# The sample rows of a decoder step: ranked over 128 partitions and finished inside the last step

## The reference, cut to what matters

```python
def peer(h, w_pq, sub_keys, u_tab, v_tab):       # 8 heads, 128 keys a side, 16384 experts
    q = (xc @ w_pq).reshape(n, 8, 2, 128)
    s = einsum('nhpd,pkd->nhpk', q, sub_keys)
    s1, i1 = top_k(s[:, :, 0], 16);  s2, i2 = top_k(s[:, :, 1], 16)
    cand = s1[..., :, None] + s2[..., None, :]   # 16 x 16 candidates a head
    top_s, pos = top_k(cand, 16)                 # 16 experts a head, 128 a token
    eid = take(i1 * 128 + i2, pos)
    g = softmax(top_s)
    act = gelu(einsum('nhkd,nd->nhk', u_tab[eid], xc))
    return einsum('nhk,nhkd->nd', g * act, v_tab[eid])

def finish(x, mixed, p, ...):
    x = x + mixed @ w_out
    x = x + peer(rmsnorm(x, norm_ffn), ...)
    gate = sigmoid(rmsnorm(x, norm_ple) @ w_ple_gate)
    return x + (p @ w_ple_proj) * gate
```

## Time and profile before

| | us |
|---|---|
| median of 3 runs (lowest, highest) | 3370.78 (3368.08, 3371.01) |
| the profiled execution | 3372.78 |
| its span, first to last instruction | 3371.1 |
| busy: DVE, PE, POOL, ACT | 2623.5, 2566.4, 1997.2, 634.9 |
| gathers (queue 0): bytes, share of 16 engines | 1082.26 MB, 80.9% |

### The profile page before, as it was taken

The page is one execution under the profiler, slowest core; times in us unless marked ns, Lnnn a source line. Parts: engine busy times, 40 slices in busy tenths (PEclk is TensorE's granted clock), DMA queues, the critical chain, the costliest instruction groups (busy, mean ns, idle before and its releaser), DMA issues.

```text
span 3371.1 us, 27956 instructions
## 1 busy us (share of the span) xinstructions
PE 2566.4 (76%) x7838; PEld 1250.0 (37%) x7838; DVE 2623.5 (78%) x5916; ACT 634.9 (19%) x1411; POOL 1997.2 (59%) x2104
## 2 busy tenths in 40 slices
PE   6898998277778777877787678767867776778768
PEld 3555545134334333433343333333433333333323
DVE  4889894988887878787878887788778877897843
ACT  2332323111111111111111111111111111121101
POOL 1000000677777777777777777777777777777672
PEclk8999998589889898989899989998998899999889
DMA  6010004899999999999999999999999999999994
GB/s 202 19 38 19 31 30 188 319 392 410 411 411 404 411 411 407 405 411 405 403 403 411 407 404 409 411 408 400 405 411 407 400 411 411 405 400 408 408 357 185
DMA packets 318210, 1144.81 MB, mean 340 GB/s; under 512 B 37648, under 2 KB 41360, under 8 KB 317040
## 3 DMA queue, kind: packets, MB, share of 16 engines
q0 software_dynamic: 297216, 1082.26, 80.9%
q1 hardware_dynamic: 20856, 60.93, 5.0%
HBM read 1133.85 MB, written 10.72 MB: 340 GB/s over the span
## 4 chain that ended last, share of the span: by engine, by line
DMA 30%; DVE 18%; POOL 17%; PE 10%; issue 8%; ACT 0%; DVEq 0%; POOLq 0%
DMA arena<-in_peer_v_dram,arena 24%; POOL arena L1078 17%; DVE arena L1327 6%; DMA arena<-in_peer_u_dram,arena 6%; PE VA L1503 6%; PE QB L1537 3%; DVE XP L1339 2%; DVE arena L1257 2%; DVE arena L1254 2%; DVE arena L1261 1%; DVE arena L1292 1%; DVE arena L1295 1%; DVE arena L1296 1%; PE QB L1483 1%; PE QB L1586 0%
## 5 line engine op out<-in xcount | busy, mean ns | idle before, releaser
L1503 PE MATMUL VA<-arena 128*128 128x512 f32 x3032 | 1628.0, 677 | 689.4 <-DMA arena<-in_peer_v_dram,arena 563.4
L1327 DVE CUSTOM_DVE_ANT_0 arena<-arena,HP 128x1024 f32<-128x1024 f32 x1024 | 1231.3, 1219 | 496.5 <-DMA arena<-in_peer_u_dram,arena 492.3
L1078 POOL DMA_INDIRECT arena<-in_peer_u_dram,arena x1032 | 990.5, 960 | 399.1 <-issue 273.5
L1078 POOL DMA_INDIRECT arena<-in_peer_v_dram,arena x1032 | 985.1, 955 | 388.5 <-issue 261.9
L1503 PEld LDWEIGHTS VA<-arena 128*128 128x128 f32 x3032 | 603.7, 214 | 1620.7 <-issue 1300.0
L1151 ACT ACTIVATE arena<-ident,arena 128x128 f32<-128x128 f32 x758 | 279.9, 396 | 1194.9 <-PE VA L1503 1188.2
L1339 DVE SCALAR_TENSOR_TENSOR XP<-arena,XP 128x1024 f32<-128x1024 f32 x258 | 332.0, 1287 | 31.7 <-DMA arena<-in_peer_v_dram,arena 24.5
L1483 PEld LDWEIGHTS QB<-arena 128*128 128x128 f32 x2304 | 268.2, 192 | 34.6 <-issue 34.6
L624 DVE SCALAR_TENSOR_TENSOR arena<-arena 128x128 f32<-128x128 f32 x960 | 273.4, 348 | 7.9
L414 POOL COPY arena<-arena 128x1024 f32<-128x1024 f32 x8 | 8.3, 1042 | 452.9 <-DVE arena L644 452.9
L1483 PE MATMUL QB<-arena 128*128 128x128 f32 x2304 | 268.6, 275 | 2.6 <-PEq L191 2.6
(11 more groups left out here) (185 smaller groups left out, 1360.4 us busy)
## 6 DMA issues: line engine op xcount, KB each, us to landing
arena<-in_peer_u_dram,arena POOLq DMA_INDIRECT x1032, 11.2
arena<-in_peer_v_dram,arena POOLq DMA_INDIRECT x1032, 11.2
arena<-x SPq DMA_DIRECT2D x17, 512.0 KB, 6.8
arena<-in_x_prompt_dram SPq DMA_DIRECT2D x16, 512.0 KB
arena<-in_peer_wq_dram SPq DMA_DIRECT2D x8, 1024.0 KB, 14.1
arena<-in_w_in_dram SPq DMA_DIRECT2D x8, 896.0 KB, 12.7
x<-arena SPq DMA_DIRECT2D x8, 512.0 KB
arena<-in_w_ple_gate_dram SPq DMA_DIRECT2D x1, 4096.0 KB, 17.2
```

The source lines that it names most:

```text
L1078: nc.gpsimd.indirect_dma_start(rows[slot(turn)], None, table, bass.IndirectOffsetOnAxis(ap=index, axis=0)).then_inc(landed[slot(turn)], 16)
L1327: nc.vector.tensor_tensor_reduce(out=row, in0=row, in1=HP[:, :], scale=1.0, scalar=0.0, op0=ALU.mult, op1=ALU.add, accum_out=dots[:, t % 2 ...
L1503: last = nc.tensor.matmul(VA[:, c:c + BANK], diag[:, n % DIAGS, :], rows[slot(turn)][:, c:c + BANK], start=v_turn(t, k) == 0, stop=v_turn( ...
```

## The change

It has four parts, all in `experts`.

1. The samples are ranked with 64 lists a side (8 tokens times 8 heads) on 128 partitions. PE makes the queries as 8-column products, four groups at `j` = 16, 19, 22, 25; one key score product a side; one ACT copy each; then one `best16` over 128 partitions, a DMA that brings the second side's lists to the first 64 partitions (`s_second`), and pairs, names and gates on 64 partitions. `idxT` is asked for at `U_SAMPLE` = 62 of step 7 in place of 114.
2. The samples' v gathers and their whole finish move from the tail into step 7 (`V_SAMPLE` = 78), as do tile 7's p turn and ple product. SP stores tile 6 and loads x of tile 7 after the samples' small DMAs in place of before them.
3. The rms scale: x is turned and multiplied without it, and the scale goes into the sigmoid's `scale`. DVE's 128x1024 scaling goes, and the finish of a tile stands 7 choices earlier.
4. Tile 7's sigmoid, product, sum and store run in two halves of 512 columns. In the tail DVE takes the odd v rows in place of the even ones.

```diff
-RANK_SAMPLE_AT = (16, 34, 68, 84)
-U_SAMPLE, V_SAMPLE = 114, 92
+U_SAMPLE, V_SAMPLE = 62, 78
-    return k % 2 == 0 if t == LAST and k >= CHOICES - LAG else k % 4 == 0
+    return k % 2 == 1 if t == LAST and k >= CHOICES - LAG else k % 4 == 0
...
 # SP
-                store(t - 1)
-                sp.wait_ge(y_stored, t * 16)
-                load_x(t)
-                load_p(SAMPLE if t == LAST else t)
+                else:
+                    store(t - 1)
+                    sp.wait_ge(y_stored, t * 16)
+                    load_x(t)
+                    load_p(t)
...
+            sp.wait_ge(sq_ready, PARTS)
             for n in range(NB):
                 sp.dma_start(h_bc[:, n, :], h_dram[n].partition_broadcast(P)).then_inc(hbc_landed, 16)
+            sp.wait_ge(s_listed, 1)
+            sp.dma_start(s_second[0:SLISTS, :], s_lists[SLISTS:2 * SLISTS, :]).then_inc(s_second_landed, 16)
+            sp.wait_ge(s_chosen_ready, 1)
+            sp.dma_start(choice_dram.rearrange("b (h k) -> (b h) k", k=TOPK), s_chosen[0:SLISTS, :]).then_inc(s_stored, 16)
             sp.wait_ge(s_stored, 2 * 16)
             sp.dma_start(idxT, choice_dram.rearrange("n c -> c n"), ...)
...
+            store(LAST - 1)
+            sp.wait_ge(y_stored, LAST * 16)
+            load_x(LAST)
+            load_p(SAMPLE)
             load_p(LAST)
             store(SAMPLE)
+            for half in range(2):
+                cols = slice(half * BANK, (half + 1) * BANK)
+                sp.wait_ge(half_ready, half + 1)
+                sp.dma_start(y_prompt[0, LAST * P:SEQ, cols], xf[:, cols]).then_inc(y_stored, 16)
...
 # ACT
+            def gate_half(half):
+                cols = slice(half * BANK, (half + 1) * BANK)
+                act.wait_ge(fin_ready, 2 * order(LAST) + 1 + half)
+                act.wait_ge(rstd_ready, order(LAST) + 1)
+                nc.scalar.activation(h3[:, cols], QB[:, cols], ACT.Sigmoid, scale=rstd2).then_inc(half_sig, 1)
...
 # DVE
-                nc.vector.tensor_scalar(h3[0:R, :], x_rows(f, R), rstd2[0:R, :], None, ALU.mult).then_inc(h3_ready, 1)
+                nc.vector.reciprocal(rstd2[0:R, :], rms2[0:R, :]).then_inc(rstd_ready, 1)
+            def sample_lists():
+                dve.wait_ge(ssc_copied, 1)
+                best16(scores[:, 0:1, 0:NKEY], values.unsqueeze(1), s_top_i.unsqueeze(1), 1, None)
+                nc.vector.tensor_copy(indices, s_top_i).then_inc(s_listed, 1)
+            def sample_pairs():                                   # at j == 38
+                dve.wait_ge(s_second_landed, 16)
...
+                best16(s_cand.unsqueeze(1), s_best.unsqueeze(1), s_best_i.unsqueeze(1), 1, None)
...
+            def finish_half(half):
+                dve.wait_ge(half_sig, half + 1)
+                steps.link(TT(ple[:, cols], ple[:, cols], h3[:, cols], ALU.mult))
+                TT(xf[:, cols], xf[:, cols], ple[:, cols], ALU.add).then_inc(half_ready, 1)
...
 # PE
+            def sample_queries(p):                                # at j == 16 + 3 * p
+                pe.wait_ge(hT_copied, SAMPLE + 1)
+                for m in range(p * LISTS, (p + 1) * LISTS):
+                    for k in range(KD):
+                        last = nc.tensor.matmul(QB[:, m * NB:(m + 1) * NB], wq[k][:, m * P:(m + 1) * P], hT[:, k, 0:NB],
+                                                start=(k == 0), stop=(k == KD - 1))
...
-            turn_h3(LAST, P)
+            turn_x2(LAST, P)
             gate_products(LAST, P)
```

More of the change, by code:

```diff
@@ L83, in count_turns @@
                     su[b], n = n, n + 1
+            if t == LAST and j == V_SAMPLE:
+                for b in range(NB):
+                    sv[b], n = n, n + 1
             u[t, j], n = n, n + 1
@@ L1094, in _ @@
                             gather(peer_u, SU_TURN[n], idxT[:, n:n + 1])
+                    if t == LAST and j == V_SAMPLE:
+                        for n in range(NB):
+                            gather(peer_v, SV_TURN[n], idxT[:, n:n + 1])
                     gather_u(t, j)
@@ L1537, in gate_product, with sample_scores @@
                     last = nc.tensor.matmul(QB[0:R, c:c + BANK], h3T[:, k, 0:R], w_gate[:, k, c:c + BANK], start=(k == 0), stop=(k == KD - 1))
-                if c and first:
+                if first:
                     last.then_inc(fin_ready, 1)
+            def sample_queries(p):
[4 more added lines that the diff above has]
+                                                start=(k == 0), stop=(k == KD - 1))
+                last.then_inc(sq_ready, 1)
+            def sample_scores():
+                pe.wait_ge(sq_copied, 1)
+                for side in range(2):
+                    last = nc.tensor.matmul(QB[side * SLISTS:(side + 1) * SLISTS, BANK:BANK + NKEY], s_q[:, side * SLISTS:(side + 1) * SLISTS],
+                                            keysT[:, side, :], start=True, stop=True)
+                last.then_inc(ssc_ready, 1)
             def gate_products(f, R):
@@ L1570, in _ @@
[L1570 to L1571 removed]
+                            turn_x2(f, P)
                         for quarter in range(4):
[L1573 removed]
+                            if j == 49 + 2 * quarter:
                                 gate_product(f, P, quarter // 2 * BANK, quarter % 2 * (KD // 2))
+                    if t == LAST:
+                        for p in range(PARTS):
+                            if j == 16 + 3 * p:
+                                sample_queries(p)
+                        if j == 30:
+                            sample_scores()
+                        if j == V_SAMPLE:
+                            pe.wait_ge(cols_ready, 1)
+                            pe.wait_ge(fin_copied, LAST)
+                            for n in range(NB):
+                                turn = SV_TURN[n]
+                                pe.wait_ge(*landing(turn))
+                                for c in range(0, D, BANK):
+                                    last = nc.tensor.matmul(QB[0:NB, c:c + BANK], w_cols[:, n, :], rows[slot(turn)][:, c:c + BANK],
+                                                            start=(n == 0), stop=(n == NB - 1))
+                                last.then_inc(s_added, 1)
+                        if j == 84:
+                            turn_p(SAMPLE, NB)
+                        if j == 87:
+                            ple_product(SAMPLE, NB)
+                        if j == 92:
+                            turn_x2(SAMPLE, NB)
+                        for quarter in range(4):
+                            if j == 96 + 2 * quarter:
+                                gate_product(SAMPLE, NB, quarter // 2 * BANK, quarter % 2 * (KD // 2))
+                        if j == 110:
+                            turn_p(LAST, P)
+                        if j == 114:
+                            ple_product(LAST, P)
```

225 lines of the change are left out of this document (124 added, 101 removed).

## The result

The changed kernel takes 3375.14 us (median of 14 runs, 3370.54 to 3384.14); beside it the kernel before took 3369.85 (14 runs). The ratio is 1.0018, with a 95% interval from 1.0009 to 1.0026: five microseconds slower, where 21.8 less were forecast. The profiled execution took 3375.08, its span 3373.3.

A forecast was written before the change was run, and what follows sets the result against it. DMA engines at 411 GB/s bound the gathers, PE after about 3310. Last landing 3320.4 plus path 28.9 gives 3349.3 against the span of 3371.1, 21.8 less; 3370.8 - 21.8 = 3349, range 3343 to 3355.

The forecast's parts named there:

- The cluster's price: Step 7, choices 16 to 25: the samples' four query groups make PE 18.6 us late; loss 0 to 12.8 us, 5 taken.
- the broadcasts: Eight 512 KB transfers SP sends after the last query group; 10.2 us of DMA time, taken to keep the engines busy.
- the ring: The 13 row buffers, 16.6 us of gathers; a user of rows may be 5.8 us late before POOL stops.
- The step's own sum: Step 7, choices 16 to 25: PE needs 30 plus 11.9 us against 23.3 of arrivals, so is 18.6 late, less 5.8.
- the queries fall to 1.2 GHz: Rival: the samples' 8-column query products lower PE's clock; 256 passes take 63 us in place of 30, time 3382; chance 0.05.
- Steps 1 to 6 ... 0, with 6 to either side: Finish of steps 1 to 6, 7 choices earlier with one DVE scaling less: 0 us change, 6 to either side.
- no wait for the samples' list: Step 7, choice 62: the list is ready with 18 us to spare, so POOL's 8.41 us wait goes.
- The second lists: Rival: in step 7 their copy queues behind the broadcasts and DVE stops at choice 38; 5 us more, 3354; chance 0.10.
- PE is in time: Tail: PE has 20 rows, 35 us of work, within 51 us of gathers.
- The path after the last landing: End of the kernel, from the last gather's landing through the final store: 28.9 us, between 25 and 32.
- its loose term: The gate product in the last path, taken as 16.88 us; 32 passes are 13.90 at the full 2.4 GHz.

## Why the prediction was wrong, point by point

Two steps failed, one that was mis-sized and one that wasn't there. With the buffer at its old place and the clock kept up, the kernel takes 3349.13 us.

**The cluster's price ("the loss is between 0 and 12.8 us; I take 5, nearer to zero because of the broadcasts").** Mechanism and place were right: PE late with v rows behind four groups, the ring giving 5.8 us, POOL stopping for the rest. The size was wrong for two reasons. First, the durations came from rows at full clock, 0.117 and 0.125 us a pass. In this cluster a pass took 8.45/64 = 0.132 to 9.83/64 = 0.154 us, and the v rows between took 5.5 to 6.0 us a pair. The step's own sum with these rows: from 2954.22 to 3006.53 PE needs 52.3 us, against 9 x 2.58 = 23.2 of arrivals; it is 29.1 late, less 5.8 is 23.3, and the stretches show 21.5 lost. Second, the broadcasts covered nothing of the first three stops: SP issues them only when the last group is done,

```profile
3006.56 6.40 SPq L1063 DMA_DIRECT2D arena<-sample_h  x8
```

in the middle of the fourth. The sentence had said so itself ("SP sends when the last group is done") and took them for cover all the same. At full clock (64 columns, old place) the same sum is 2984.9 - 2945.9 = 39.0 less 23.2 less 5.8 = 10.0, and the stretches show 8.2. So at full clock the sum of this step holds, and 8.2 lies inside its 12.8; the 5 taken was too little, and the price of the clock came on top: 14.6 us by one pair of runs, 14.2 by the other.

**The rival "the queries fall to 1.2 GHz".** It named the cause, products of 8 columns, and had 0.05. The full price was too high: the granted clock went to 0.57 in the worst 10 us and to 0.67 to 0.77 over stretches of 25 that PE filled, in the three kernels with 8 columns, not to 0.5 throughout, and a pass reached 0.154 us where the rival needed 0.2. That its 3382 lies near the 3375.14 measured is luck: 11.8 us of the measured time are the layout's, which it did not have. The reason given against the rival, the 8-column passes of the earlier trace rows, was 16 passes in one place; they don't tell what 64 in a row, four times over, do to the clock. It also forgot that v rows between the groups pay as well. Of the two sections of the Trainium skill that the prediction weighed (TensorE: Matmul & The Clock Gate), the passes at full clock side with LDWEIGHTS: 7.25/64 = 0.113 us with 64 columns and 0.116 with 8, against the 0.107 worked out from it, and not with the 0.025 of Back-to-back issue gap. (The trace's record of a single load is 0.19 us, longer than the pitch from one to the next, so the records overlap; what is compared is the pitch.)

**What had no step: the layout.** "Steps 1 to 6 ... 0, with 6 to either side" looked at the finish, and the finish is neutral as it said (3373.34 with it put back). The drift was in the list of tiles: one row buffer moved off a multiple of 256 bytes. It costs 11.8 us in the changed kernel; the layout of the change costs 10.4 in the kernel before. No row of before names it, but there was something to ask: all the buffers' starts can be worked out from the tiles' sizes, and the prediction took "411 GB/s" for a constant of the machine, while it was that of twelve buffers off the multiple and one on it. The Trainium skill, DMA: Bandwidth & Descriptors, section How a descriptor splits into AXI transactions, has a rule that bears on it: a transfer is cut into pieces of 256 bytes, which start on multiples of 256, so that one that starts elsewhere takes a piece more. By that a row of 4096 bytes takes 17 pieces in place of 16, an estimate of 6.3% from that page. For the one buffer the runs agree in direction and nearly in size: 8971 against 9009 packets are 0.42%, for one buffer in thirteen, so 5.5% for the buffer that moved. For the other twelve they agree in direction only: 2.1% came out (9201 against 9009 packets), so 2.1 x 13/12 = 2.3% for each. So the runs show the price of the place; that the pieces are the reason they don't show, and what holds the engines at 420 GB/s with every buffer on the multiple stays open. (The expectations of the runs on the multiple took POOL's issue for the next bound; their ranges came true, that reason did not.)

**What was right.** POOL has no wait for the samples' list: it is loaded at 3058.87 and lands 14.2 us later. The second lists don't queue behind the broadcasts: SP sent the last of those at about 3013 and the copy at 3025.36, when nearly all their bytes had moved, and DVE did not wait for it. The copy took 5.3 us to land, as the DMA issues of the changed kernel from 3000 to 3090 us show (count, KB each, median us to landing):

```profile
arena<-sample_h SPq DMA_DIRECT2D x8, 512.0 KB, 8.9
...
arena<-arena SPq DMA_DIRECT2D x1, 8.0 KB, 5.3
...
arena<-sample_choices SPq DMA_DIRECT2D x1, 4.0 KB, 14.2
```

That rival is out, since its condition did not come about; what a small copy right behind the broadcasts would meet, no run here shows. In the tail POOL does not stop and PE is in time. The path after the last landing was forecast at 28.9 us and is 28.7, with the gate product, its loose term, at 16.98 (16.88 taken).

**The sum again.** 3349 forecast, 11.8 for the layout, 14.2 for the clock: 3375.0, measured 3375.14. Since 11.8 and 14.2 are differences between runs, this says no more than that the run with both undone took 3349.13, as forecast. That is nearer than its steps deserve: its cluster lost 8.2 where 5 were taken, and its last path is 26.5 us (3321.17, the last DVE row, to 3347.7) where 28.9 were, the gate product being 15.66. These two cancel to a microsecond, by luck.

## What to carry to other kernels

Read the list of tiles in a diff as closely as its instructions: work out where each buffer that a DMA fills starts, since a tile added somewhere else can move it off a multiple of 256 bytes, and here 32 bytes of filler were worth 53.6 us, where the change was to bring 21.8. Let the start of a buffer be one of the things that a measured bandwidth may hang on. Take a duration only from a row in the same surroundings: passes of 8 columns packed together lowered PE's granted clock for themselves and for the work between them, and padding them to 64 columns was the cheaper way, by 14 to 16 us. And when something is to cover a stall, check in the order of the queues that it is issued before the stall and not by what ends it.

## What the runs showed that I had not expected

- **Gathers of 4 KB rows are slower into buffers that start off a multiple of 256 bytes,** by 5.5% for the one buffer moved by itself and some 2.3% for each of the other twelve. 3370 us with twelve of thirteen buffers off, 3380 with thirteen, 3317 with none; 64 and 128 past are as slow as 224 past, within 6 us.
- **PE's granted clock fell while PE was busy all the time.** With 8 columns a product it was 0.84, 0.57, 0.77, 0.84, 0.70 and 0.66 in the six stretches of 10 us from 2950 to 3010, in each of which PE was busy for 10.00 us; the chip's levels being 1.2 and 2.4 GHz, such a value is a mixture of both. With 64 columns it was 0.94 or more from 2950 to 3000. The clock followed the width of the products, not the busy share. With four packs of 16 products of 8 columns in place of four of 64, the packs ran at 1.00. Why, no run shows.
- **A wider product took less time.** 64 passes of 64 columns took 7.25 us, 64 passes of 8 columns 8.45 to 9.83. It is the clock and not the width that does it: at full clock a pass of 8 columns took 0.116 us and one of 64 took 0.113.
- **POOL's issue is the next bound, just above,** 0.94 us and 0.30 between two, 421 GB/s for gathers of 512 KB. With all buffers on the multiple the DMA engines make 420, so work on the layout has little more to give here unless POOL's issues become fewer or shorter.
